# A fused encoder layer: moving waits, copies and one table load in the mix stage and first gate pair

## The chip, the cores and the metric

The kernel is one program on one core of a Trainium2 chip. The core has TensorE (PE: matmuls into PSUM, with the weight loads PEld beside them), VectorE (DVE), ScalarE (ACT), GpSimd (POOL) and SyncE (SP), whose queue issues nearly all DMA transfers here. The engines run their own instruction streams and meet at semaphores. The metric is the device time in microseconds, the median of several executions.

## The reference

One encoder layer in fp32 is computed for two sequences of 1024 and 512 tokens, width 1024:

```python
u = rms_norm(h, g_norm)
z = u @ w_in                      # q, k, v, attention gate, recurrent input, its gate
o_att = diff_attention(q, k, v, ...)      # 8 heads, softmax difference, rms_norm per head
o_lru = rg_lru_branch(xr, ...)            # conv, two gated scans
mix = concat([o_att * silu(g_att), o_lru * silu(g_lru)])
h = h + mix @ w_out
e = (p @ w_ple) * sigmoid(h @ w_pg)
h = h + rms_norm(e, g_ple)
```

## The kernel before

The 1536 tokens are 12 tiles of 128. Products are made from a high and a low fp32r part of each operand, three matmuls for one. The stages follow each other: projections, recurrent branch, attention (96 steps, the last near 745 us), then the mix stage and the gate stage, which the change touches.

In the mix stage, position n of twelve takes tile SEQ[n], SEQ = 0, 1, 2, 8, 9, 3, 10, 4, 11, 5, 6, 7. Its steps are these. SP's load_o(n) (L862) reads the tile's attention output from DRAM into one of two buffers o_in. square_o(n) on ScalarE (L1473) squares it, mean_square(n) on VectorE (L1982 to L1989) sums, scales and inverts, root_o and scale_o(n) on ScalarE (L1477, L1484) give O_n, with eight scalings. turn_o(n) on TensorE (L2474) transposes O_n. o_gate(n) on VectorE (L1996) multiplies with the gate Gt that load_mix(n) (L868) has fetched into its one buffer, mix_high(n) on ScalarE (L1468) and mix_low(n) on VectorE (L2003) split the result. mix_product(n) on TensorE (L2212 to L2214) is 24 matmuls with wa, and add_x(n) on VectorE (L2022) adds the residual row. For tiles 0 to 7 (HALF: eight positions, n = 0, 1, 2, 5, 7, 9, 10, 11) the recurrent half of the product was made in the attention stage and stored to hpart; SP loads it (load_hp) with x (load_x_again), and GpSimd adds them (add_half, L1119). For tiles 8 to 11 (WHOLE: n = 3, 4, 6, 8) TensorE makes that half here, from mf and wl (L2436 to L2438, half_tile, 12 matmuls each, two for a tile); the first of them, at n = 3, is made ahead. TensorE takes turn_o(n + 1) ahead of mix_product(n), and so ahead of the half tiles in it.

Beside this the gate's weights are prepared: load_wg (L814) fetches eight blocks of 512 KB of w_pg in two halves, gate_sum and gate_low on VectorE (L2026) and gate_high on ScalarE (L1488) form sums and high and low parts, one or two for a position, each of 128 x 2048 elements. The gate product is of Strassen's kind: for each of six pairs of tiles, seven products p1, p5, p6, p7, p3, p4, p2 (L2537 to L2540) in place of eight. TensorE keeps each sum in PSUM and ScalarE's copy_sum (L1596) saves p1, p5 and p6 before the next adds to the same bank. a11, a22, a12 and s1 to s4 are quarters of the transposed h and their sums; *_high on ScalarE (L1533, L1541, L1547, L1556) and *_low on VectorE and GpSimd (L1137) split them.

The order on each engine is written out by hand. A wait blocks all that stands behind it on its engine; the order of SP's queue (L918 to L964) is the order in which the transfers are requested. A pair's products wait as follows: p6 for the low part of s2, for the copy of p1 and for weights; p7 for the copy of p6. a22_high(0) waits for add_x(11), since a22 lies where hp_sb was. load_o(n) waits for scale_o(n - 2); load_o(3) also for the last store of attention output (store_o(1, 3), L779). In the lists for ScalarE (L1564) and VectorE (L2078) the loop over n goes through the positions.

Of the kernel before, what the change touches and what calls it, by code (L numbers as in the profile page):

```python
# [26 lines left out]
ACT = mybir.ActivationFunctionType  # L27
# [8 lines left out]
NT = T // P  # L36
NB = T // 512
HEADS, HV, HQ = 8, 64, 32
# [34 lines left out]
def encoder_layer(nc, x, x_t, p_in, g_norm, w_in, w_cols, norms, lams, rel_bias, onehot, chan, w_a, w_x,  # L73
# [20 lines left out]
    with ctx:  # L94
# [486 lines left out]
        def _(sp):  # L581
# [193 lines left out]
            def store_o(u, i):  # L775

                n_tok, first = UNITS[u]
                sp.wait_ge(o_done, 4 * i + 3 + u)
                sp.dma_start(o_tok[first:first + n_tok, ds(P * i, P)].rearrange("(t p) c -> p t c", p=P),  # L779
                             O_at[i % 2][:, first // P:(first + n_tok) // P, :]).then_inc(o_st[i % 2], 16)  # L780
# [24 lines left out]
            def store_hp(j):  # L805
                sp.wait_ge(hp_done, j + 1)
                sp.dma_start(hpart[j // 2 * P:(j // 2 + 1) * P, j % 2 * 512:(j % 2 + 1) * 512], hp[:, j % 2, :]
                             ).then_inc(hp_out[j % 2], 16)
                if j % 2 and j // 2 + 2 < NT:
                    load_mf(j // 2 + 2)  # L810

            def load_wg(half):
                for k in range(4 * half, 4 * half + 4):
                    sp.dma_start(wg_raw[:, k, :], w_pg[k * P:(k + 1) * P, :]).then_inc(wg_in[half], 16)  # L814
# [43 lines left out]
            def load_o(n):  # L858
                if n >= 2:
                    sp.wait_ge(fin["o_norm"], n - 1)  # L860
                t = SEQ[n]
                sp.dma_start(o_in[n % 2][:], o_tok[t * P:(t + 1) * P, :]).then_inc(fin[f"o_in{n % 2}"], 16)  # L862

            def load_mix(n):
                if n:
                    sp.wait_ge(fin["mixed"], n)
                t = SEQ[n]
                sp.dma_start(Gt[:], z_ch[P:, t * P:(t + 1) * P].rearrange("(c r p) t -> p c r t", r=3, p=P)[:, :, 2, :]  # L868
                             ).then_inc(fin["g_in"], 16)
# [57 lines left out]
            load_o(1)  # L927
            load_hp(0)
            load_hp(1)
            sp.wait_ge(s_mm, 2 * NSTEP)  # L930
            load_wg(1)
            store_hp(IN_STEPS - 2)
            load_mix(1)
            store_hp(IN_STEPS - 1)
            for b in range(2):
                sp.wait_ge(hp_out[b], 16 * IN_STEPS // 2)
            load_x_again(1)
            load_o(2)
            store_o(1, HEADS // 2 - 1)
            load_mf(10)  # L940
            for n in range(NT):
                if n == 0:
                    load_mix(n + 2)
                    sp.wait_ge(o_st[1], 16 * 4)
                if n + 3 < NT:
                    load_o(n + 3)
                if 1 <= n < NT - 2:
                    load_mix(n + 2)
                if 1 <= n < NT - 1:
                    load_x_again(n + 1)  # L950
                    if n + 1 in HALF and HALF.index(n + 1) >= 2:
                        load_hp(HALF.index(n + 1))
                if 1 <= n <= IN_DRAM:
                    store_h(n - 1)
                if n == 4:
                    load_mf(11)
                if n == 8:
                    sp.wait_ge(f_mm, 2 * NT)
                    for k in range(PC):
                        sp.dma_start(wp_raw[:, k, :], w_ple[k * P:(k + 1) * P, :]).then_inc(wp_in, 16)  # L960
                if n == 9:
                    load_p(0, 1)
                    load_p(0, 0)
# [222 lines left out]
        def _(act):  # L1186
# [327 lines left out]
            mix_high(0)  # L1514
            heads_out(2 * HEADS - 1)
            square_o(2)
            mix_high(1)

            def a21_copy(g):
# [42 lines left out]
                act.activation(p_hi[:, r, :, :], p_sb[:, r, :, :], ACT.Copy).then_inc(fin["p_hi"], 1)  # L1562

            for n in range(NT):  # L1564
                if n == 0:
                    root_o(2)
                    scale_o(2)
                if n + 3 < NT:
                    square_o(n + 3)
                if 1 <= n < NT - 1:  # L1570
                    mix_high(n + 1)
                if 1 <= n < NT - 2:
                    root_o(n + 2)
                    scale_o(n + 2)
                if n in (0, 1, 2, 3, 4, 6, 8):
                    gate_high({0: 0, 1: 1, 2: 2, 3: 3, 4: 4, 6: 5, 8: 6}[n])
                if n == NT - 3:
                    for k in range(PC):
                        act.wait_ge(wp_in, 32)
                        act.activation(wp_hi[:, k, :], wp_raw[:, k, :], ACT.Copy).then_inc(wp_hi_done, 1)  # L1580
# [4 lines left out]
            sum_high(0, 1, s3_raw, s3, "p7")  # L1585
            sum_high(0, 2, s1_raw, s1, "p5")
            sum_high(0, 3, s2_raw, s2, "p6")
            a22_high(0)
            a12_high(0)
            sum_high(0, 4, s4_raw, s4, "p3")  # L1590

            def copy_sum(g, name, ps, at, free):
                act.wait_ge(fin["g_mm"], START["g_mm"] + step_of(name, g))
# [23 lines left out]
            for g in range(PAIRS):  # L1617
                if g:
                    gate_sigmoid(g - 1, 3, sg[0][:, LEFT])
                copy_sum(g, "p1", left_ps[:], sg[0][:, LEFT], 0)  # L1620
                if g:
                    square_e(g - 1, 0)
                copy_sum(g, "p5", right_ps[:], sg[1][:, RIGHT], 1)
                copy_sum(g, "p6", left_ps[:], sg[0][:, RIGHT], 0)
                if g < LAST:
                    a21_copy(g + 1)
                gate_sigmoid(g, 1, sg[1][:, RIGHT])
                gate_sigmoid(g, 2, sg[0][:, RIGHT])
                if g == LAST:
                    break  # L1630
                a11_high(g + 1)
                sum_high(g + 1, 1, s3_raw, s3, "p7")
                left_sigmoid(g)
                a22_high(g + 1)
                sum_high(g + 1, 2, s1_raw, s1, "p5")
                sum_high(g + 1, 3, s2_raw, s2, "p6")
                square_e(g, 1)
                a12_high(g + 1)
                sum_high(g + 1, 4, s4_raw, s4, "p3")
                p_high(g + 1, 1)  # L1640
                p_high(g + 1, 0)
# [9 lines left out]
        def _(dve):  # L1651
# [397 lines left out]

            def gate_weights(n):  # L2050

                if n < 3:
                    gate_sum(n)
                if n == 3:
                    gate_low(wg_hi[:, TOP, LEFT], wg_lo[:, TOP, LEFT], wg_raw[:, TOP, LEFT], 1, 1)
                if n == 4:
                    gate_low(t1_hi[:], t1_lo[:], t1_raw[:], 2, 3)
                if n == 5:
                    gate_low(wg_hi[:, TOP, RIGHT], wg_lo[:, TOP, RIGHT], wg_raw[:, TOP, RIGHT], 4, 2)
                if n == 6:  # L2060
                    gate_low(wg_hi[:, BOTTOM, RIGHT], wg_lo[:, BOTTOM, RIGHT], wg_raw[:, BOTTOM, RIGHT], 3, 3)
                if n == 8:
                    gate_sum(3)
                    gate_low(t2_hi[:], t2_lo[:], t2_raw[:], 5, 4)
                if n == 9:
                    gate_low(wg_hi[:, BOTTOM, LEFT], wg_lo[:, BOTTOM, LEFT], wg_raw[:, BOTTOM, LEFT], 6, 4)
                if n == 10:
                    gate_low(t4_hi[:], t4_lo[:], t4_raw[:], 7, 4)
# [9 lines left out]
            for n in range(NT):  # L2078
                if 1 <= n < NT - 1:
                    o_gate(n + 1)  # L2080
                if n:
                    add_x(n - 1)
                if 1 <= n < NT - 1:
                    mix_low(n + 1)
                if n + 3 < NT:
                    mean_square(n + 3)
                gate_weights(n)

            def sum_three(g):
                dve.wait_ge(fin["t_act"], 4 * g + 1)  # L2090
# [112 lines left out]
        def _(pe):  # L2203
# [273 lines left out]
            def mix_product(n, between=None):  # L2477
                if n == 1:
                    pe.wait_ge(wt_done, NSTEP)
                    pe.wait_ge(o_done, 2 * HEADS)  # L2480
                if n == 2 or n >= 4:
                    pe.wait_ge(fin["h_done"], {2: 1, 4: 2, 5: 3}.get(n, n - 1))
                if n in WHOLE[1:]:
                    half_tile(2 * SEQ[n])
                    half_tile(2 * SEQ[n] + 1)
                pe.wait_ge(fin["m_lo"], n + 1)
                for b in range(2):
                    c = slice(b * 512, (b + 1) * 512)
                    mm = product(mix_bank(n)[:, b, :], [(m_hi[n % 2][:, k, :], m_lo[n % 2][:, k, :], wa_hi[:, k, c],
                                                         wa_lo[:, k, c]) for k in range(LC)], start=n in HALF)  # L2490
                    if between and b == 0:
                        between()
                mm.then_inc(fin["h_mm"], 1)
# [114 lines left out]
            pe.wait_ge(wa_lo_done, LC)  # L2608
            mix_product(0, second_tile)
            for n in range(1, NT - 1):  # L2610
                turn_o(n + 1)
                mix_product(n)
            turn_a21(0)
            turn_a11(0)
# [70 lines left out]
```

## Time and profile before

| | |
|---|---|
| median of 3 executions | 1032.72 us (1032.64 to 1032.97) |
| profiled execution | 1032.86 us, span 1031.1 us |
| TensorE busy | 991.2 us, 96% |
| VectorE, ScalarE, GpSimd busy | 671.5, 638.0, 483.5 us |
| chain that ended last | PE 70%, DVE 15%, issue 8%, ACT 3% |
| DMA | 154.55 MB, mean 150 GB/s |

Times in the rows are microseconds from the span's start. A row of the timeline has start, duration, engine, line, operation, what it writes and reads, and in brackets the idle time of the engine before it with what ended it. The last of the attention stage is near 745 us, the mix stage runs from there to 855 us, the gate stage to the end.

### The profile page before, as it was taken

How to read it: one execution, taken by the hardware profiler on the slowest of the kernel's cores; microseconds unless marked ns; L12 is line 12 of the kernel's file. 1: busy time of each engine (PE TensorE's matmuls, PEld its weight loads, DVE VectorE, ACT ScalarE, POOL GpSimd, SP SyncE). 2: the span in 40 equal slices, each digit the busy share in tenths (PEclk: the TensorE clock that was granted, in tenths of full speed). 3: DMA queues.
4: the chain of work that ended last, by engine and by line, in shares of the span. 5: the costliest groups of instructions: out<-in, count | busy, mean ns of one | idle time of the engine just before them, and what ended most of it. 6: DMA issues, size and time to landing. Idle time of an engine off the chain costs nothing.

```text
span 1031.1 us, 15665 instructions
## 1 busy us (share of the span) xinstructions
PE 991.2 (96%) x5720; PEld 786.0 (76%) x5720; DVE 671.5 (65%) x1118; ACT 638.0 (62%) x1050; POOL 483.5 (47%) x396
## 2 busy tenths in 40 slices
PE   8999999999999999989999999999988997999996
PEld 7867777777788888878777777777766886888875
DVE  4645857592583341579999999999857562444444
ACT  7748485846632232579999999999746442444442
POOL 1163343626666540155676677666610135554451
PEclk9999999999999999999999999999999998999998
DMA  9651543323256437669866657623557680122222
GB/s 346 260 151 36 174 148 103 118 82 133 75 178 185 134 102 207 199 167 241 210 174 172 176 160 180 155 64 139 176 175 235 206 274 10 41 92 81 84 72 82
DMA packets 106908, 154.55 MB, mean 150 GB/s; under 512 B 10312, under 2 KB 69192, under 8 KB 106824
## 3 DMA queue, kind: packets, MB, share of 16 engines
q1 hardware_dynamic: 106688, 153.55, 49.7%
q8 instruction: 46, 0.75, 0.3%
q14 instruction: 30, 0.25, 0.1%
q10 hardware_dynamic: 144, 0.00, 0.0%
HBM read 104.17 MB, written 46.20 MB: 146 GB/s over the span
## 4 chain that ended last, share of the span: by engine, by line
PE 70%; DVE 15%; issue 8%; ACT 3%; DMA 2%; POOL 2%; SPq 0%; DVEq 0%; ACTq 0%; POOLq 0%
DVE E_ L1905 10%; PE b_ps L2350 6%; PE b_ps L2352 6%; PE b_ps L2351 6%; PE b_ps L2212 6%; PE b_ps L2214 5%; PE b_ps L2213 5%; PE o_ps L2407 3%; PE s_ps L2363 3%; PE w_ps L2324 3%; PE uT_ps L2287 2%; PE left_ps L2537 2%; PE left_ps L2540 2%; PE left_ps L2539 2%; DVE ratio L1914 2%
## 5 line engine op out<-in xcount | busy, mean ns | idle before, releaser
L1387 ACT ACTIVATE E_<-E_,nmax 128x1024 f32<-128x1024 f32 (+1 forms) x184 | 186.5, 1018 | 13.2 <-DVE nmax L1905 13.2
L1905 DVE CUSTOM_DVE_ANT_0 E_<-s_ps,bias 128x1024 f32<-128x1024 f32 (+1 forms) x184 | 188.2, 1057 | 9.8 <-PE s_ps L2363 9.6
L1089 POOL TENSOR_TENSOR E_<-E_,ratio 128x576 f32<-128x576 f32 (+3 forms) x92 | 84.5, 919 | 92.8 <-DVE E_ L1921 92.8
L1092 POOL TENSOR_TENSOR E_<-E_ 128x576 f32<-128x576 f32 (+3 forms) x92 | 103.6, 1126 | 7.2
L2214 PE MATMUL b_ps<-u_hi,wA_lo 128*128 128x512 f32 x256 | 99.8, 390 | 0.0
L2363 PE MATMUL s_ps<-KL,QL 128*128 128x512 f32 x256 | 88.6, 430 | 8.1 <-DVE nmax L1905 8.0
L1402 ACT ACTIVATE WT<-w_ps 128x1024 f32<-128x1024 f32 (+1 forms) x96 | 83.5, 870 | 5.9 <-PE w_ps L2324 5.5
L2212 PE MATMUL b_ps<-u_hi,wA_hi 128*128 128x512 f32 x216 | 85.5, 396 | 0.0
L2324 PE MATMUL w_ps<-ident,E_ 128*128 128x128 f32 x624 | 83.5, 273 | 2.1 <-ACT WT L1402 2.0
L2324 PEld LDWEIGHTS w_ps<-ident,E_ 128*128 128x128 f32 x624 | 72.5, 140 | 15.2 <-issue 6.3
L2213 PE MATMUL b_ps<-u_lo,wA_hi 128*128 128x512 f32 x216 | 84.1, 389 | 0.0
L2407 PE MATMUL o_ps<-WT,V 128*64 128x128 f32 x1280 | 84.0, 278 | 0.0
L2407 PEld LDWEIGHTS o_ps<-WT,V 128*64 128x64 f32 x1280 | 68.5, 136 | 18.6 <-issue 18.6
L1000 POOL TENSOR_TENSOR rsq<-msq,neghalf 128x16 f32<-128x16 f32 x24 | 69.7, 2902 | 2.0
L1921 DVE SCALAR_TENSOR_TENSOR E_<-E_,ratio 128x448 f32<-128x448 f32 (+4 forms) x92 | 66.0, 718 | 3.2
L2350 PE MATMUL b_ps<-wB_hi,u_hi 128*128 128x512 f32 x168 | 66.8, 398 | 0.0
L2352 PE MATMUL b_ps<-wB_hi,u_lo 128*128 128x512 f32 x168 | 65.6, 390 | 0.0
L2351 PE MATMUL b_ps<-wB_lo,u_hi 128*128 128x512 f32 x168 | 65.4, 389 | 0.0
L1356 ACT ACTIVATE z_stage<-b_ps 128x512 f32<-128x512 f32 x24 | 14.3, 595 | 80.2 <-PE b_ps L2352 80.2
L1119 POOL TENSOR_TENSOR hp_sb<-hp_sb,x_rd 128x1024 f32<-128x1024 f32 x8 | 21.7, 2712 | 80.8 <-DMA hp_sb<-hpart 75.7
L1865 DVE TENSOR_REDUCE ssq<-z_stage 128x16 f32<-128x512 f32 x24 | 16.4, 683 | 66.0 <-ACT z_stage L1356 66.0
L2363 PEld LDWEIGHTS s_ps<-KL,QL 128*128 128x128 f32 x256 | 40.3, 189 | 20.7 <-DVE nmax L1905 17.2
(345 smaller groups left out, 2590.7 us busy)
## 6 DMA issues: line engine op xcount, KB each, us to landing
QL<-qk_t SPq DMA_DIRECT2D x32, 256.0 KB, 7.3
KL<-qk_t SPq DMA_DIRECT2D x32, 256.0 KB, 8.5
bias<-line_d SPq DMA_DIRECT2D x8, 960.0 KB, 11.8
x_sb<-in_x SPq DMA_DIRECT2D x12, 512.0 KB, 9.2
z_ch<-z_stage SPq DMA_DIRECT2D x24, 256.0 KB, 3.3
qk_t<-qh SPq DMA_DIRECT2D x24, 256.0 KB, 2.3
qk_t<-ql SPq DMA_DIRECT2D x24, 256.0 KB, 2.8
mf<-mix_t SPq DMA_DIRECT2D x24, 256.0 KB, 5.2
```

Of the source, the lines that this page charges most:

```text
L1092: gp.tensor_tensor(one, one, two, ALU.add).then_inc(w_gp, 1)
L1387: act.activation(e, e, ACT.Exp, bias=nmax[:, n % 5, c:c + 1], scale=-1.0, accum_out=sums[:, n % 5, c:c + 1]).then_inc(e_done, 1)
L1905: dve.tensor_tensor_reduce(weights_at(n)[:, c, 0:n_tok], s_ps[:, c, 0:n_tok], b[:, ::-1], -1.0, 3e38, ALU.add, ALU.min, nmax[:, n % 5, c:c ...
L2212: pe.matmul(dst, sh, mh, start=start and k == 0, stop=False)
L2213: pe.matmul(dst, sh, ml, start=False, stop=False)
L2214: mm = pe.matmul(dst, sl, mh, start=False, stop=k == n - 1)
L2324: mm = pe.transpose(w_ps[:, k, :], weights_at(n)[:, 0, k * P:(k + 1) * P], ident[:])
L2350: pe.matmul(dst, u_hi[:, b, k, c], wB_hi[g][:, k, :], start=k == 0, stop=False)
L2351: pe.matmul(dst, u_hi[:, b, k, c], wB_lo[g][:, k, :], start=False, stop=False)
L2352: mm = pe.matmul(dst, u_lo[:, b, k, c], wB_hi[g][:, k, :], start=False, stop=k == KC - 1)
L2363: mm = pe.matmul(s_ps[:, c, b * 512:(b + 1) * 512], q_tile(u, hh)[:, c, qt * P:(qt + 1) * P], k_tile(u, hh)[:, c, b * 512:(b + 1) * 512], ...
L2407: mm = pe.matmul(o_ps[HV * j:HV * j + HV, 0, pair * P:(pair + 1) * P], V_at[i % 2][:, first // P + k, HV * (head % 2):HV * (head % 2) + HV ...
```

## The change

- SP: load_o(2) goes from behind load_x_again(1) to right behind load_mix(1), ahead of two stores. store_o(1, 3) goes ahead of the waits on hp_out and load_x_again(1). load_wg(1), with its wait, goes from ahead of store_hp(14) into the loop at n = 0, behind load_o(3).
- ScalarE: one added activation, a Sqrt of one element for each partition, between square_o(2) and mix_high(1). In the loop mix_high(n + 1), root_o(n + 2) and scale_o(n + 2) stand ahead of square_o(n + 3), where the square stood first. In the first pair a22_high(0), a12_high(0) and sum_high(0, 4) go behind the copies of p1 and p5.
- VectorE: gate_sum(1) and gate_sum(2) go from n = 1 and 2 to n = 2 and 3, the first gate_low from 3 to 1; gate_weights(n) stands ahead of mean_square(n + 3).
- TensorE: at n = 4, 6 and 8 turn_o(n + 1) goes behind the half tiles, ahead of the rest of mix_product(n).

```diff
--- SP
             load_hp(1)
-            sp.wait_ge(s_mm, 2 * NSTEP)
-            load_wg(1)
             store_hp(IN_STEPS - 2)
             load_mix(1)
+            load_o(2)
             store_hp(IN_STEPS - 1)
+            store_o(1, HEADS // 2 - 1)
             for b in range(2):
                 sp.wait_ge(hp_out[b], 16 * IN_STEPS // 2)
             load_x_again(1)
-            load_o(2)
-            store_o(1, HEADS // 2 - 1)
             load_mf(10)
...
                     load_o(n + 3)
+                if n == 0:
+                    sp.wait_ge(s_mm, 2 * NSTEP)
+                    load_wg(1)
--- ScalarE
             square_o(2)
+            act.activation(mse[:, 0:1], neghalf[:, 0:1], ACT.Sqrt, scale=-2.0)
             mix_high(1)
...
             for n in range(NT):
-                if n == 0:
-                    root_o(2)
-                    scale_o(2)
+                if 1 <= n < NT - 1:
+                    mix_high(n + 1)
+                if n + 2 < NT:
+                    root_o(n + 2)
+                    scale_o(n + 2)
                 if n + 3 < NT:
                     square_o(n + 3)
-                if 1 <= n < NT - 1:
-                    mix_high(n + 1)
-                if 1 <= n < NT - 2:
-                    root_o(n + 2)
-                    scale_o(n + 2)
...
             sum_high(0, 3, s2_raw, s2, "p6")
-            a22_high(0)
-            a12_high(0)
-            sum_high(0, 4, s4_raw, s4, "p3")
...
                 copy_sum(g, "p5", right_ps[:], sg[1][:, RIGHT], 1)
+                if g == 0:
+                    a22_high(0)
+                    a12_high(0)
+                    sum_high(0, 4, s4_raw, s4, "p3")
                 copy_sum(g, "p6", left_ps[:], sg[0][:, RIGHT], 0)
--- VectorE
-                if n < 3:
-                    gate_sum(n)
-                if n == 3:
+                if n in (0, 2, 3):
+                    gate_sum((0, None, 1, 2)[n])
+                if n == 1:
                     gate_low(wg_hi[:, TOP, LEFT], wg_lo[:, TOP, LEFT], wg_raw[:, TOP, LEFT], 1, 1)
...
+                gate_weights(n)
                 if n + 3 < NT:
                     mean_square(n + 3)
-                gate_weights(n)
--- TensorE
                     half_tile(2 * SEQ[n] + 1)
+                    turn_o(n + 1)
...
             for n in range(1, NT - 1):
-                turn_o(n + 1)
+                if n not in WHOLE[1:]:
+                    turn_o(n + 1)
                 mix_product(n)
```

## Rows read from the trace of the kernel before

**Rows 1.** The page's first part: busy us, share of the span, instructions of each engine.

```profile
PE 991.2 (96%) x5720; PEld 786.0 (76%) x5720; DVE 671.5 (65%) x1118; ACT 638.0 (62%) x1050; POOL 483.5 (47%) x396
```

**Rows 2.** Timeline of TensorE: start, duration, line, operation, idle before and releaser.

```profile
765.06 0.65 PE L2474 MATMUL t_ps<-ident,O_n 128*128 128x128 f32 x4 [4.20 <-ACT O_n L1484]
...
782.25 0.66 PE L2474 MATMUL t_ps<-ident,O_n 128*128 128x128 f32 x4 [3.36 <-ACT O_n L1484]
...
836.49 0.60 PE L2474 MATMUL t_ps<-ident,O_n 128*128 128x128 f32 x4
...
842.52 0.60 PE L2474 MATMUL t_ps<-ident,O_n 128*128 128x128 f32 x4
...
867.58 0.77 PE L2537 MATMUL left_ps<-t_hi,s_hi 128*128 128x512 f32 x1 [5.53 <-issue]
```

**Rows 3.** Stretches: length, busy time (instructions) by engine, granted clock, DMA share, GB/s.

```profile
740.00:746.00 6.00, 6.00 (x54) 4.74 (x52) 3.59 (x3) 2.05 (x2) 5.24 (x5) 1.00 1.01 402
...
765.00:769.00 4.00, 3.94 (x13) 3.21 (x14) 3.37 (x5) 2.96 (x4) 0.00 (x0) 0.60 0.22 66
...
782.20:785.60 3.40, 3.35 (x11) 2.72 (x12) 3.40 (x3) 2.46 (x3) 0.00 (x0) 0.59 0.33 87
...
867.50:871.50 4.00, 3.92 (x9) 3.15 (x10) 0.00 (x0) 0.47 (x1) 0.84 (x1) 0.50 0.00 0
```

**Rows 4.** Timeline of ScalarE in the mix stage, same columns.

```profile
758.11 0.63 ACT L1473 ACTIVATE O_sq<-o_in 128x512 f32<-128x512 f32 x1 [8.76 <-DMA o_in<-o_tok]
760.81 0.63 ACT L1468 ACTIVATE m_hi<-mr 128x512 fp32r<-128x512 f32 x1 [2.06 <-DVE mr L1996]
761.46 1.28 ACT L1477 ACT_TABLE_LOAD   x1
...
778.90 0.63 ACT L1473 ACTIVATE O_sq<-o_in 128x512 f32<-128x512 f32 x1 [4.75 <-DMA o_in<-o_tok]
...
837.91 0.64 ACT L1468 ACTIVATE m_hi<-mr 128x512 fp32r<-128x512 f32 x1 [1.45 <-DVE mr L1996]
...
838.67 2.03 ACT L1484 ACTIVATE O_n<-o_in,rso 128x64 f32<-128x64 f32 x8
```

**Rows 5.** Timeline of SP's queue: start and duration of each issue of a transfer.

```profile
747.63 0.38 SPq L868 DMA_DIRECT2D Gt<-z_ch  x1
...
751.96 0.43 SPq L862 DMA_DIRECT2D o_in<-o_tok  x1
...
753.70 0.37 SPq L779 DMA_DIRECT2D o_tok<-O  x1
...
761.26 0.45 SPq L862 DMA_DIRECT2D o_in<-o_tok  x1
```

**Rows 6.** DMA issues of 736:739, 739.4:739.6, 753.6:754, 761.2:761.5: count, KB, us to landing.

```profile
wg_raw<-in_w_pg SPq DMA_DIRECT2D x4, 512.0 KB, 8.6
...
hpart<-hp SPq DMA_DIRECT2D x1, 256.0 KB, 9.0
...
o_tok<-O SPq DMA_DIRECT2D x1, 512.0 KB, 7.3
...
o_in<-o_tok SPq DMA_DIRECT2D x1, 256.0 KB, 3.1
```

**Rows 7.** VectorE's stretch (busy, clock, DMA, GB/s); timeline of GpSimd and VectorE at 743.

```profile
805.10:811.10 6.00, 5.62 (x7) 1.00 0.67 227
...
743.12 2.37 POOL L1119 TENSOR_TENSOR hp_sb<-hp_sb,x_rd 128x1024 f32<-128x1024 f32 x1
743.19 2.85 DVE L1974 TENSOR_TENSOR O_n<-o_in,rso 128x512 f32<-128x512 f32 x1 [2.37 <-POOL rso L1112]
```

**Rows 8.** Timeline of GpSimd and ScalarE in the first pair, same columns.

```profile
856.39 3.79 POOL L1137 TENSOR_TENSOR s_lo<-s_raw,s_hi 128x512 fp32r<-128x512 f32 x3 [1.59 <-ACT s_hi L1556]
...
860.13 2.39 POOL L1119 TENSOR_TENSOR hp_sb<-hp_sb,x_rd 128x1024 f32<-128x1024 f32 x1
...
866.89 0.59 ACT L1596 ACTIVATE sg<-left_ps 128x512 f32<-128x512 f32 x1
```

## The prediction

> **What bounds the kernel now.** Read the busy shares first: TensorE is busy 991.2 us of a span of 1031.1 [rows 1]. So only idle or slow stretches of TensorE can be won. Next read TensorE's timeline for rows with an idle time before them, from the last attention steps (735 us) to the end. Three are over 0.7 us. The turn of the third output tile waits 4.20 us for O_n, the turn of the fifth waits 3.36 us for O_n, and product p6 of the first pair starts after 5.53 us without a releaser that the profile names [rows 2]. Then read the stretches for the granted clock. Behind each of the three gaps the clock is at its lower level, 1.2 GHz, for part of the stretch: mean 0.60 over 4.0 us, 0.59 over 3.4 us, 0.50 over 4.0 us [rows 3]. TensorE stays busy there and does less, so a gap also costs 4.0 x 0.40 = 1.6, 3.4 x 0.41 = 1.4 and 4.0 x 0.50 = 2.0 us. The three together hold 13.1 us of idle time and 5.0 of slow clock, 18.1 us. All else in this part of TensorE's timeline is back to back.
>
> **The third tile (first gap).** ScalarE's rows show the order of the delay: square_o(2) waited 8.76 us for the transfer of o_in(2) and ran at 758.11, and behind it lie the VectorE chain, mix_high(1), a table load of 1.28 us, the root and eight scalings [rows 4]. The transfer was issued at 751.96, fifth after Gt(1) at 747.63 [rows 5]. The change issues it right behind Gt(1), at 748.05. A load of this size landed in 3.1 us [rows 6], so it lands at 751.2; even with the 9.0 us of a transfer behind 2 MB it would be there at 757.1. VectorE cannot take it before 753.7 (heads_scaled), and its three small steps end by 755. The extra Sqrt makes the table load run while ScalarE is idle until 758.1 [rows 4]. It fits in those 8.76 us, so I cost it at nothing; if a second load were to come behind it, that would be 1.28 us more.
> What is late next is the turn of tile 1 at 757.47, which is not moved. From a turn to m_hi is 1.42 us (836.49 to 837.91), and from m_hi's start to the end of O_n is 2.79 us (837.91 to 838.67 + 2.03) [rows 2, 4]. So m_hi(1) starts at 758.9 and O_n(2) ends at 761.7. TensorE runs out of work at 765.06 - 4.20 = 760.86. New gap: 0.85 us.
>
> **The fourth and fifth tiles.** A half-tile step of TensorE lasts 6.03 us (836.49 to 842.52) [rows 2], so the turn of tile 3 is due at 761.7 + 6.0 = 767.7. load_o(3) waits for the store of heads 6 and 7 (issued 753.70, landed 7.3 us later at 761.0, with three transfers beside it). One of these has now gone ahead and x_rd(1) comes behind, so the store no longer decides; mixed(2) at 758.9 does. The request leaves at 759.3 in place of 761.26 [rows 5]. In front of it are the two mf transfers of load_mf(10) and Gt(2), so I take 763.3 and not 759.3 + 3.1 = 762.4 [rows 6]. Where a square is what VectorE waits for, m_hi starts 2.7 us behind the square's start (758.11 to 760.81, with one turn between) [rows 4]; taking 2.6, m_hi(2) is at 765.9 and O_n(3) ends at 768.7: a gap of 0.95 us where there was none. Between 0.1 us (landing 762.4) and 2.4 us (landing 764.8).
> Behind load_o(3) now go the four loads of the gate weights, 2 MB, from 759.7. SP's queue stands 2.5 us longer, and load_o(4), load_mix(3), load_x_again(2), load_hp(2), store_h(0) and load_o(5) queue behind it. The rows price this: weights land 8.6 us after issue, and the 256 KB store behind them in the kernel before took 9.0, against 3.1 us for a free queue [rows 6]. The first weights were then behind 1.5 MB of other loads; now only Gt(2) and o_in(3) are ahead. 2.1 MB at the 402 GB/s of that time [rows 3] are 5.2 us. From 762.9, when o_in(3) is through, that puts the end of the weights at 768.1 and o_in(4) at 769.3, with its own 0.6 us and 0.6 to the semaphore (estimate; 771.4 with the full 9.0 from 762.4). square_o(4) starts with ScalarE free at 768.7, so 769.3; m_hi(3) is at 771.9 and O_n(4) ends at 774.7, both by the same two spans. Turn 4 is due at 768.7 + 6.0 = 774.7. Gap 0 to 0.1, up to 2.1 with the late landing. The 3.36 us gap there came from square_o(5) standing ahead of mix_high(3) and waiting 4.75 us for its transfer [rows 4]; with squares last, a late o_in(5) meets a step with 5.5 us more to give, because tile 9's half products now run ahead of the turn.
> Sum: 4.20 + 3.36 + 1.6 + 1.4 = 10.6 us go, 0.85 + 0.95 + 0.05 = 1.85 come, gain 8.7.
>
> **The later tiles.** At three whole tiles (positions 4, 6, 8) the turn moves behind 24 half products, 5.5 us nearer to its product. From turn to O_n of the next tile is 1.42 + 2.79 = 4.2 us against 6.03 us: 1.8 us of cover at positions 4 and 6. At position 8 VectorE has two gate steps of 2.25 us each between that turn and mean_square(11), which was ahead of them before: the chain is 12.4 us for two steps of 12.1. I take 0.2 us. SP's load_mix waits for that turn's o_gate, so loads of x, hp and w_ple leave up to 5.5 us later at positions 4, 6 and 8. The last additions of GpSimd (2.39 us each [rows 8]) may then hold add_x(10): 0 to 1.5 us, I take 0.3.
>
> **The first pair (third gap).** Follow the rows back. p6 starts at 867.58, right behind ScalarE's copy of p1 at 866.89. p1 had ended by 858.9; the copy stood behind a22_high, which waited for add_x(11), which waited for GpSimd's addition at 860.13 to 862.52, which stood behind three s_lo from 856.39 [rows 2, 8]. The change puts copies p1 and p5 ahead of a22_high. p6 then needs the third s_lo (856.39 + 3.79 = 860.2), copy p1 (859.6) and the end of p5 at 862.05: no gap. Next late are the embedding product at 864.9 (its p_lo ends by 864.0) and p7 at 868.1, which needs the copy of p6; ScalarE gets to that at 867.0, after the same high parts as before, and is done at 867.5. Cover 0.6 us. Gain 5.53 + 2.0 = 7.5 us; all of p6 to the end moves with it. If the cover fails, what a22_high lacks falls on p7.
>
> **Sum.** 8.7 - 0.2 - 0.3 + 7.5 = 15.7 us. The profiled execution took 1032.86 us (span 1031.1), 0.14 over the median of 1032.72. 1032.72 - 15.7 = 1017.0 us. Ends of the unknown costs: with no new gap at all 1014.6; with the late values at tiles 3 and 4 (1.5 + 2.0) and add_x(10) (1.2) 1021.7.
>
> **Rivals.**
> A. The 2 MB in the queue make a new gap. For it: 9.0 against 3.1 us [rows 6], and eight transfers behind. Against: a step to spare. o_in(4) 2.1 us later and o_in(5) or hp(2) late enough for one more 2 us, with one clock drop of 1.6 [rows 3]: 1017.0 + 5.5 = 1022.5. Chance 0.14.
> B. The reordered copies only shift the wait to p7, because GpSimd's last addition lands late (it follows all SP loads that now leave later). Then the 7.5 are not won: 1024.5. Chance 0.08.
> C. VectorE becomes the bound, and the kernel is slower. In a half-tile step with a gate step it is busy 5.62 of 6.00 us [rows 7], and mean_square now stands behind the gate step, so that nothing is left in between. The place is GpSimd's addition of hp and x: at 743.12 it ran 2.37 us, and VectorE's O_n begun at 743.19 took 2.85 us, until it was over [rows 7], where this size takes 0.69. If in each of the eight half-tile steps an addition met a VectorE subtraction first, a step would last 5.62 + 2.39 = 8.0 us: 8 x 2.0 = 15.8 us, and with three clock drops of 1.5 the time is 1017.0 + 20.3 = 1037.3. It makes the kernel slower from 2.0 us per step on. Against it: the additions now fall on PSUM reads and reductions in most steps. Chance 0.04. The Trainium skill, SBUF — State Buffer, section "Who interferes with whom", states this as a rule: a VectorE operation with two SBUF inputs and a GpSimd one that reads SBUF exclude each other, and the second waits for the whole first. By that rule the moved subtractions (two SBUF inputs) speak against this change, with the time of C at full overlap; the row at 743.19 agrees.
> The forecast itself: 0.72. Something else: 0.02.
>
> **How the numbers follow.** The forecast's own range is 1014 to 1020. With rival A and the late bounds it reaches to 1023; B and C, 0.12, are left out with what lies under 1013.8. A measurement of this kernel can tell about 0.2% (2 us) from no change. The forecast, A and B are all faster: 0.93. Within 0.2% needs B with A: 0.03. Slower: 0.04.
>
> **What would show it.** Right: m_hi(1) near 758.9 with no table load behind it; turn 2 at 761.7 with 0.9 us idle before it; turns 3 and 4 with idle times under 1 us each; full granted clock from 760 to the end of the pair stage; p6 directly behind p5; the turn at the first whole tile 5.5 us behind its half products' start. Wrong: an O_sq row that waits for o_in over 3 us at tile 4; an idle time before p7 or the embedding product; VectorE's m_lo or gate rows of over 2.5 us; an idle time before the turns of tiles 10 and 11.

## The result

| | us | ratio to the kernel before, 95% interval |
|---|---|---|
| kernel before | 1032.68 | |
| changed kernel | 1017.84 | 0.9853 (0.9834 to 0.9873) |
| the same once more, another chip run | 1017.93, beside 1031.86 | 0.9869 (0.9849 to 0.9888) |

The forecast was 1017.0 us, the range 1013.8 to 1023.0. The time fell by 14.8 us in the first set and by 13.9 in the second; 15.7 were forecast. The profile below is of one execution of the second set, 1020.3 us with a span of 1018.5. (The first set has four executions, and the one profiled took 1975.09 us, with TensorE busy for 99% of it at a recorded clock of 1.00, and cannot be compared: the median of 1017.84 counts it, the ratio is that of the other three, and their median is 1017.26, 15.4 us below the kernel before.)

The first part of the page after, beside [rows 1], has 2.8 us less of busy TensorE and a shorter span:

```profile
span 1018.5 us, 15666 instructions
PE 988.4 (97%) x5720; PEld 783.9 (77%) x5720; DVE 672.2 (66%) x1118; ACT 638.5 (63%) x1051; POOL 486.9 (48%) x396
```

The timeline of TensorE after, the rows that answer to [rows 2], in brackets the idle time before one: the turns of positions 2, 3 and 11, the turn of h for a12, p6, the turn behind it, and p7. The turn of position 3 is new among them; L2511 turns h for the first pairs.

```profile
761.32 0.66 PE L2474 MATMUL t_ps<-ident,O_n 128*128 128x128 f32 x4 [0.87 <-ACT O_n L1485]
...
770.19 1.12 PE L2474 MATMUL t_ps<-ident,O_n 128*128 128x128 f32 x4 [2.62 <-ACT O_n L1485]
...
836.69 0.66 PE L2474 MATMUL t_ps<-ident,O_n 128*128 128x128 f32 x4
...
850.28 0.66 PE L2511 MATMUL t_ps<-ident,h_sb 128*128 128x128 f32 x4 [0.45 <-DVE a_lo L2026]
...
856.36 0.39 PE L2538 MATMUL left_ps<-t_hi,s_hi 128*128 128x512 f32 x1
...
861.88 0.60 PE L2511 MATMUL t_ps<-ident,h_sb 128*128 128x128 f32 x4
862.23 0.48 PE L2538 MATMUL left_ps<-wg_hi,s_hi 128*128 128x512 f32 x1
```

p6 starts at 856.36, directly behind p5 (the row at 867.58 in [rows 2] had 5.53 us before it), and the turn behind p6 and its embedding product follows after 5.52 us. The timeline of ScalarE after, its table load and the two squares that waited, against [rows 4]:

```profile
751.00 0.63 ACT L1474 ACTIVATE O_sq<-o_in 128x512 f32<-128x512 f32 x1 [2.04 <-DMA o_in<-o_tok]
751.65 1.28 ACT L1518 ACT_TABLE_LOAD   x1
...
758.48 0.63 ACT L1469 ACTIVATE m_hi<-mr 128x512 fp32r<-128x512 f32 x1 [5.33 <-DVE mr L1996]
759.02 0.19 ACT L1478 ACTIVATE rso<-rso 128x8 f32<-128x8 f32 x1
759.25 2.02 ACT L1485 ACTIVATE O_n<-o_in,rso 128x64 f32<-128x64 f32 x8
764.87 0.63 ACT L1474 ACTIVATE O_sq<-o_in 128x512 f32<-128x512 f32 x1 [3.60 <-DMA o_in<-o_tok]
...
768.12 2.02 ACT L1485 ACTIVATE O_n<-o_in,rso 128x64 f32<-128x64 f32 x8
```

The square of tile 2 runs 7.1 us earlier than before, the table load lies in idle time, and O_n(2) ends at 761.27 with the turn at 761.32. But the square of tile 3 now waits 3.60 us for its transfer, and O_n(3) ends at 770.14. TensorE had been idle since 767.57: 2.62 us. Stretches of the kernel after, as in [rows 3], with us, the busy time of TensorE, its weight loads, VectorE, ScalarE and GpSimd, the granted clock, the DMA share and GB/s: this gap, what follows, and the rest up to the end of the mix stage.

```profile
767.50:770.10 2.60, 0.07 (x1) 0.00 (x0) 2.60 (x3) 2.57 (x10) 0.00 (x0) 0.99 0.83 290
770.10:773.50 3.40, 3.31 (x10) 2.83 (x11) 3.22 (x6) 2.78 (x4) 0.00 (x0) 0.50 0.95 286
773.50:855.00 81.50, 81.00 (x374) 65.50 (x374) 52.73 (x62) 41.87 (x103) 25.07 (x11) 1.00 0.66 222
```

So one slow stretch is left, 3.4 x 0.50 = 1.7 us, where there were three. The transfers behind the gap, against [rows 6], are o_in(3) issued at 758.94, Gt(2) at 758.48, o_in(4) at 761.56 and the last store of heads at 753.30, with KB and us to landing:

```profile
o_in<-o_tok SPq DMA_DIRECT2D x1, 256.0 KB, 5.9
...
Gt<-z_ch SPq DMA_DIRECT2D x1, 256.0 KB, 5.4
...
o_in<-o_tok SPq DMA_DIRECT2D x1, 256.0 KB, 9.1
...
o_tok<-O SPq DMA_DIRECT2D x1, 512.0 KB, 5.2
```

### The profile page after: what moved, and what is told of

Same layout as the page of the kernel before. It is cut to its first block, busy times and chain, and to the rows that moved or that the text cites. A ratio compares the mean times of both kernels' runs of the same rounds, so it can differ in the third digit from the quotient of the medians.

```text
span 1973.3 us, 15666 instructions
## 1 busy us (share of the span) xinstructions
PE 1963.0 (99%) x5720; PEld 1239.4 (63%) x5720; DVE 671.7 (34%) x1118; ACT 652.2 (33%) x1051; POOL 471.0 (24%) x396
## 4 chain that ended last, share of the span: by engine, by line
PE 99%; DVE 0%; ACT 0%; issue 0%; DVEq 0%; POOL 0%; POOLq 0%
PE s_ps L2363 8%; PE o_ps L2407 8%; PE w_ps L2324 8%; PE b_ps L2352 6%; PE b_ps L2351 6%; PE b_ps L2350 6%; PE b_ps L2212 6%; PE b_ps L2213 6%; PE b_ps L2214 6%; PE left_ps L2540 2%; PE uT_ps L2287 2%; PE left_ps L2538 2%; PE left_ps L2541 2%; PE right_ps L2541 2%; PE h_ps L2212 2%; PE h_ps L2214 2%
## 5 line engine op out<-in xcount | busy, mean ns | idle before, releaser
L2214 PE MATMUL b_ps<-u_hi,wA_lo 128*128 128x512 f32 x256 | 172.6, 674 | 0.0
L2324 PE MATMUL w_ps<-ident,E_ 128*128 128x128 f32 x624 | 169.0, 439 | 0.0
L2407 PE MATMUL o_ps<-WT,V 128*64 128x128 f32 x1280 | 157.8, 444 | 0.0
L2363 PE MATMUL s_ps<-KL,QL 128*128 128x512 f32 x256 | 153.6, 718 | 0.0
L2213 PE MATMUL b_ps<-u_lo,wA_hi 128*128 128x512 f32 x216 | 145.8, 675 | 0.0
L2212 PE MATMUL b_ps<-u_hi,wA_hi 128*128 128x512 f32 x216 | 145.3, 673 | 0.0
L2350 PE MATMUL b_ps<-wB_hi,u_hi 128*128 128x512 f32 x168 | 114.9, 684 | 0.0
L2214 PEld LDWEIGHTS b_ps<-u_hi,wA_lo 128*128 128x128 f32 x256 | 75.4, 294 | 41.7 <-issue 39.2
L2212 PEld LDWEIGHTS b_ps<-u_hi,wA_hi 128*128 128x128 f32 x216 | 65.0, 301 | 53.2 <-issue 50.4
L2213 PEld LDWEIGHTS b_ps<-u_lo,wA_hi 128*128 128x128 f32 x216 | 64.3, 298 | 33.4 <-issue 30.8
```

Source lines behind the costliest of these rows:

```text
L2212: pe.matmul(dst, sh, mh, start=start and k == 0, stop=False)
L2213: pe.matmul(dst, sh, ml, start=False, stop=False)
L2214: mm = pe.matmul(dst, sl, mh, start=False, stop=k == n - 1)
L2324: mm = pe.transpose(w_ps[:, k, :], weights_at(n)[:, 0, k * P:(k + 1) * P], ident[:])
L2350: pe.matmul(dst, u_hi[:, b, k, c], wB_hi[g][:, k, :], start=k == 0, stop=False)
L2363: mm = pe.matmul(s_ps[:, c, b * 512:(b + 1) * 512], q_tile(u, hh)[:, c, qt * P:(qt + 1) * P], k_tile(u, hh)[:, c, b * 512:(b + 1) * 512], ...
```

## Experiments

Each is compared with the kernel before, run beside it on the same chip. The theory is the prediction's: three gaps and the clock behind them are what is won. Rivals A (the 2 MB of gate weights in the queue), B (the copies only move the wait) and C (VectorE becomes the bound) stand against it. Where an edit is to the changed kernel, "the whole" is that kernel. The sets ran on different chips. The kernel before took 1031.86 us beside the first four of the kernels below, 1032.36 beside the next four, 1033.02 beside the three after them and 1032.33 beside the last, and within a set its executions lie up to 4.9 us apart. So across sets the gains over the kernel before are what is compared (the whole: 13.9 us), and differences of 1 to 2 us are not read as effects. Each kernel has one trace, and what a trace shows is that one execution.

**The whole change again.** (Run whole.)

> The whole change once more, for its profile. My theory: 1017.0 us; idle time of TensorE 0.85 us before the turn of tile position 2, 0.95 us (0.1 to 2.4) before position 3, under 0.1 (up to 2.1) before position 4, 0.2 before position 11, none before p6, and the granted clock at its upper level from 760 us to the end of the pair stage. The rival in which the 2 MB of gate weights hold the queue: a gap of over 2 us before position 4 with a stretch of lower clock behind it, 1022 us. The rival in which the copies shift the wait: idle time before p7.

Measured 1017.93 us. The gap before turn 2 was 0.87 us, before turn 3 2.62, before turn 4 none, before turn 11 about 0.2 (836.69 where 6.03 us behind 830.44 is 836.47), before p6 and p7 none. A wait that I had not seen stood before the turn of a12, 0.45 us. Rival B's mark is absent. The gap of over 2 us with a stretch of lower clock, which was to be rival A's mark at position 4, came at position 3.

**The first pair's copies alone.** The kernel before with this edit is pair_only:

```diff
             sum_high(0, 3, s2_raw, s2, "p6")
-            a22_high(0)
-            a12_high(0)
-            sum_high(0, 4, s4_raw, s4, "p3")
...
                 copy_sum(g, "p5", right_ps[:], sg[1][:, RIGHT], 1)
+                if g == 0:
+                    a22_high(0)
+                    a12_high(0)
+                    sum_high(0, 4, s4_raw, s4, "p3")
```

> The kernel before with only the three high parts of the first pair put behind the copies of p1 and p5. My theory: the gap of 5.53 us before p6 and the slow clock of 2.0 us behind it go, 7.5 us: 1025.2. The first two gaps stay at 4.20 and 3.36. If the wait only shifts to p7: 1032.7.

Measured 1024.82 against 1031.86: 7.0 us, ratio 0.9931 (0.9911 to 0.9952). The gap before p6 is gone from the timeline of TensorE and the first gap stands nearly as before, 3.93 us (the second 3.49):

```profile
764.38 0.66 PE L2475 MATMUL t_ps<-ident,O_n 128*128 128x128 f32 x4 [3.93 <-ACT O_n L1484]
```

**Everything else alone.** The whole with this edit taken back is mix_only.

> The change without the reordered copies of the first pair. My theory: 8.7 - 0.5 = 8.2 us are won, 1024.5, with the gap of 5.5 us before p6 still there. If the parts are worth less together than alone, the sum of the two single gains is over the gain of the whole.

Measured 1025.51: 6.4 us, ratio 0.9938 (0.9919 to 0.9957). In the timeline of TensorE the gap before p6 is back, 5.56 us:

```profile
861.17 0.77 PE L2537 MATMUL left_ps<-t_hi,s_hi 128*128 128x512 f32 x1 [5.56 <-issue]
```

7.0 + 6.4 = 13.4 us, and the whole gave 13.9. Within the intervals the parts add up. The pair's part is the larger one, and the mix stage fell short of the forecast's 8.2.

**Gate weights in their old place.** Run wg_early is the whole, with

```diff
             load_hp(1)
+            sp.wait_ge(s_mm, 2 * NSTEP)
+            load_wg(1)
             store_hp(IN_STEPS - 2)
...
-                if n == 0:
-                    sp.wait_ge(s_mm, 2 * NSTEP)
-                    load_wg(1)
```

> The whole change, but the second half of the gate weights requested in its old place, ahead of the hpart stores. It tells what the 2 MB cost where they stand now. My theory: with them gone from behind load_o(3), o_in(4) lands 5 us earlier, but turn 4 waits for the chain of squares that starts at turn 3 either way, so the time falls by 0 to 0.5 us against the whole change (1016.5 to 1017). If the 2 MB make a gap of their own, it falls by 2 us or more.

Measured 1017.64 us, ratio 0.9860 (0.9841 to 0.9880): no difference from the whole that the timing can tell. In its timeline the gap before turn 3 is 1.52 in place of 2.62, with no slow stretch behind it, and that before the turn of a12 is 1.34 in place of 0.45 (VectorE waited 2.35 us for gpB, see below); o_in(3) landed at 763.99 in place of 764.85. Of the 1.10 us saved in one place 0.89 were waited for in the other. The 1.10 us cannot be put down to the 2 MB: in gain_late (below), with the 2 MB where the whole has them, the gap is 1.72 us. The two rows, first of wg_early (this kernel), then of gain_late:

```profile
769.33 0.65 PE L2473 MATMUL t_ps<-ident,O_n 128*128 128x128 f32 x4 [1.52 <-ACT O_n L1484]
...
769.42 0.66 PE L2475 MATMUL t_ps<-ident,O_n 128*128 128x128 f32 x4 [1.72 <-ACT O_n L1485]
```

**load_o(3) first.** Run o3_first is the whole, with SP's order

```diff
             store_o(1, HEADS // 2 - 1)
+            sp.wait_ge(o_st[1], 16 * 4)
+            load_o(3)
+            load_mix(2)
             for b in range(2):
                 sp.wait_ge(hp_out[b], 16 * IN_STEPS // 2)
             load_x_again(1)
             load_mf(10)
             for n in range(NT):
-                if n == 0:
-                    load_mix(n + 2)
-                    sp.wait_ge(o_st[1], 16 * 4)
-                if n + 3 < NT:
+                if 1 <= n and n + 3 < NT:
                     load_o(n + 3)
```

> The whole change with load_o(3) and load_mix(2) ahead of load_x_again(1) and load_mf(10) in SP's queue. In the trace of the whole change o_in(3) took 5.91 us to land behind x_rd(1), two mf transfers and Gt(2), and turn 3 waited 2.62 us. If what stands ahead in the queue is the cause, it lands in 3 to 4 us, by 762, the gap before turn 3 falls under 0.3 us, no stretch of lower clock is left, and 1.5 to 3.5 us are won where a drop is avoided (1015 to 1016). If the 2 MB behind it are the cause, it stays over 1.5 us.

Measured 1021.29 us, ratio 0.9890 (0.9870 to 0.9909): 11.1 us are won, 2.9 less than by the whole. The two intervals overlap; on the same chip in the same set the whole with only the wait for the gains moved took 1017.45 us, 3.8 us less. Half of the expectation held. o_in(3) landed in 2.7 us and the gap before turn 3 is gone. But the next load, behind the 2 MB, took 9.7 us, the square of tile 4 waited 5.76 us for it, and the gap came back larger before turn 4. The DMA issues of o_in(3) and o_in(4) in o3_first, with KB and us to landing:

```profile
o_in<-o_tok SPq DMA_DIRECT2D x1, 256.0 KB, 2.7
...
o_in<-o_tok SPq DMA_DIRECT2D x1, 256.0 KB, 9.7
```

And in the timeline of the same kernel the square that waited and turn 4:

```profile
771.73 0.63 ACT L1474 ACTIVATE O_sq<-o_in 128x512 f32<-128x512 f32 x1 [5.76 <-DMA o_in<-o_tok]
...
777.04 1.11 PE L2474 MATMUL t_ps<-ident,O_n 128*128 128x128 f32 x4 [4.03 <-ACT O_n L1485]
```

This is rival A's mechanism, in full view once the gap ahead of it no longer covers it (the next but one experiment takes the 2 MB away, and the gap goes). In the whole change o_in(4) lands just as late (9.1 us), but turn 3 is then 2.6 us late itself, so turn 4 does not wait. The 2 MB cost so little there because something else was late first. One thing this edit does not separate: it moves o_in(3) away both from what stood ahead of it and from the 2 MB behind it.

**The wait for the gains later.** The row below is from the timeline of VectorE in the whole. It waited for gpB, the gain row of the last norm, which is not used before the first pair's end.

```profile
848.17 0.69 DVE L2026 TENSOR_TENSOR s_raw<-t_ps,a_raw 128x512 f32<-128x512 f32 x1 [1.32 <-DMA gpB<-in_g_ple]
```

The edit on VectorE (run gain_late):

```diff
-            dve.wait_ge(gain_in, 32)
             sum_three(0)
...
                     joined(g - 1, 3, "p2", right_ps[:], sg[0][:, LEFT])
+                    if g == 1:
+                        dve.wait_ge(gain_in, 32)
                     scaled_e(g - 1, 1)
```

> The whole change with VectorE's wait for the gains gpB moved from ahead of the first pair's sums to the first use. In the trace of the whole change VectorE waited 1.32 us for this transfer, and the turn of a12 waited 0.45 us for a_lo. If the transfer is the cause, both go and 0.3 to 0.5 us are won in TensorE's timeline (less than the timing can tell). If the chain through add_x(10) is as late, the 0.45 stay.

Measured 1017.45 us, ratio 0.9865 (0.9849 to 0.9881). The wait and the 0.45 us before the turn of a12 are gone; the gain, 14.9 us, differs from the whole's by less than the runs scatter.

**The three together.** load_o(3) first, weights in their old place, late wait for the gains (run best).

> Both of these, with the second half of the gate weights in its old place ahead of the hpart stores (as in the run before, where that left the time unchanged). If the three terms add up, no gap of TensorE over 0.9 us is left in the mix stage and at the first pair: 0.87 before turn 2 and nothing else. 1018 - 2.6 - 0.5 = 1015, and down to 1013.5 where the clock drop of 1.6 was in the median. If the loads crowd each other again it stays at 1017 to 1018.

Measured 1015.62 us (1015.33 to 1015.98), ratio 0.9840 (0.9826 to 0.9855). Only 0.87 us before turn 2 is left in the mix stage. o3_first and this kernel ran in one set and differ by 5.7 us, with intervals that do not touch. They differ in the place of the weights and the wait for the gains; the second removed 0.45 us where it stood alone, so the place of the weights is worth about 5 us here. Their traces agree: a gap of 4.03 us and a slow stretch of 1.7 are gone. In the whole change the same place was worth nothing that could be measured.

**Without the added Sqrt.** Run no_sqrt is the whole, with

```diff
-            act.activation(mse[:, 0:1], neghalf[:, 0:1], ACT.Sqrt, scale=-2.0)
```

> The whole change without the added Sqrt of one column. The table load of 1.28 us comes back between m_hi(1) and the root. My theory: turn 2 waits 2.15 us in place of 0.87, but turn 3 is bound by o_in(3) and not by this, so its gap shrinks by the same 1.28 us: the time stays within 0.5 us. If the table load had a longer cost (2.66 us by the page ScalarE: Activation LUTs of the Trainium skill, section What ACT_TABLE_LOAD costs, which counts a drain with it), turn 2 would wait 3.5 us.

Measured 1018.3 us, ratio 0.9865 (0.9850 to 0.9880), no difference from the whole. Rows of its timeline, ScalarE and turn 2 of TensorE:

```profile
758.93 0.63 ACT L1469 ACTIVATE m_hi<-mr 128x512 fp32r<-128x512 f32 x1 [6.71 <-DVE mr L1995]
759.58 1.28 ACT L1478 ACT_TABLE_LOAD   x1
760.88 0.21 ACT L1478 ACTIVATE rso<-rso 128x8 f32<-128x8 f32 x1
...
763.19 1.12 PE L2473 MATMUL t_ps<-ident,O_n 128*128 128x128 f32 x4 [2.29 <-ACT O_n L1485]
```

The load costs 1.28 us and the step behind it starts at once: the gap is 2.29 us, 1.4 more than with the Sqrt, and not 3.5. No gap is left before turn 3, which is due 3.1 us later: 1.4 for the longer gap and 1.7 for a slow stretch behind turn 2. So what came later in one place was paid out of the next gap, as expected, and by more than the 1.28 us expected.

**The square first on ScalarE.** Run square_first is the whole, with the old order in the loop:

```diff
+                if n == 0:
+                    root_o(2)
+                    scale_o(2)
+                if n + 3 < NT:
+                    square_o(n + 3)
                 if 1 <= n < NT - 1:
                     mix_high(n + 1)
-                if n + 2 < NT:
+                if 1 <= n < NT - 2:
                     root_o(n + 2)
                     scale_o(n + 2)
-                if n + 3 < NT:
-                    square_o(n + 3)
```

> The whole change, but in ScalarE's loop the square of position n + 3 again ahead of mix_high and the root and scalings. My theory: square_o(5) waits for o_in(5), which lands near 778, and holds m_hi(3) and O_n(4), so turn 4 waits about 5 us and a stretch of lower clock follows: 4 to 7 us over the whole change, 1022 to 1025. If the order on ScalarE did not matter once the requests are early, the time stays at 1018.

Measured 1023.6 us, ratio 0.9909 (0.9892 to 0.9925): 9.4 us are won, 4.5 less than by the whole, and 5.3 less than by the next kernel, which ran beside it. The size was right and the place wrong by one tile: it is square_o(4), not square_o(5), that holds m_hi(2) and O_n(3), and turn 3 waits, as its timeline shows.

```profile
768.95 0.63 ACT L1474 ACTIVATE O_sq<-o_in 128x512 f32<-128x512 f32 x1 [3.36 <-DMA o_in<-o_tok]
769.49 0.61 ACT L1469 ACTIVATE m_hi<-mr 128x512 fp32r<-128x512 f32 x1
...
772.30 1.12 PE L2477 MATMUL t_ps<-ident,O_n 128*128 128x128 f32 x4 [5.84 <-ACT O_n L1485]
```

**The turns at whole tiles early.** Run turn_early is the whole, with turn_o(n + 1) again ahead of the half tiles at positions 4, 6 and 8.

```diff
                     half_tile(2 * SEQ[n] + 1)
-                    turn_o(n + 1)
...
-                if n not in WHOLE[1:]:
-                    turn_o(n + 1)
+                turn_o(n + 1)
```

> The whole change, but at positions 4, 6 and 8 the turn of the next tile again ahead of the half products. In the trace of the whole change O_n(5) ended at 783.25 while product 3 ended near 782.1: turn 5 would wait 1 to 1.5 us, the other two nothing, and the last turns lose their 0.2. So 0.5 to 1.5 us slower, near what the timing can tell. If the cover of 5.5 us was needed at all three places, 3 us or more.

Measured 1018.28 us, ratio 0.9860 (0.9846 to 0.9875). There is one gap of 0.70 us more, before turn 5, and the gain of 14.7 us is not distinguishable from the whole's. So this part of the change is not shown to be worth anything here.

**mean_square ahead of the gate step.** Run gates_after is the whole, with VectorE's two steps in the old order.

```diff
-                gate_weights(n)
                 if n + 3 < NT:
                     mean_square(n + 3)
+                gate_weights(n)
```

> The whole change, but VectorE's mean_square(n + 3) again ahead of the gate step. VectorE then waits for the square with the gate step behind it: o_gate(3) starts 2.3 us later and turn 4 waits about 2.3 us, with a clock drop of 1.6 at most; at position 8 the 0.2 us before turn 11 change little. 1 to 4 us slower: 1019 to 1022. If VectorE has room either way, 1018.

Measured 1023.05 us, ratio 0.9906 (0.9883 to 0.9929): 10.0 us are won, 4.0 less than by the whole and 4.8 less than by the kernel with the early turns, which ran beside it. The interval just overlaps the whole's and does not touch that kernel's. The time is 1 us over the highest that I had written. gate_sum(0), 2.3 us, already stands behind the wait of mean_square(3), so turn 3 and not turn 4 waits, 4.02 us; turn 11 waits 1.77 us, since the two gate steps at position 8 now begin only when the square of tile 11 is there (at 831.29, against 827.44 in the whole). The two turns in its timeline:

```profile
771.29 1.12 PE L2474 MATMUL t_ps<-ident,O_n 128*128 128x128 f32 x4 [4.02 <-ACT O_n L1485]
...
839.47 0.66 PE L2474 MATMUL t_ps<-ident,O_n 128*128 128x128 f32 x4 [1.77 <-ACT O_n L1485]
```

Against the whole's trace these two gaps are 1.4 and 1.5 us longer, 3 us together; the rest of the difference in the medians no trace explains.

**Turn 1 ahead of the second half tile.** On top of the three together (run best_turn1):

```diff
             def second_tile():
-                half_tile(IN_STEPS + 1)
                 turn_o(1)
+                half_tile(IN_STEPS + 1)
```

> The version with load_o(3) first, the gate weights in their old place and the late wait for the gains, and on TensorE the turn of tile 1 ahead of the 12 half products of tile 8's second half instead of behind them. My theory: turn 1 comes 2.7 us earlier, so m_hi(1) and O_n(2) do, and the last gap in the mix stage, 0.87 us before turn 2, goes; what is late next is o_in(3), which lands at 759.7: 1015.6 - 0.9 = 1014.7. If O_n(2) is held by something else (the square or the mean of tile 2), the gap stays and the time is 1015.6.

Measured 1014.88 us (1013.68 to 1014.89), ratio 0.9826 (0.9799 to 0.9852). No gap of TensorE is left from the attention's end to the second pair but 0.2 us before p5. The gain over the kernel before is 17.5 us against 16.7 for the three together; a difference of 0.7 us, about what was expected, but within the scatter.

Not tried alone are load_o(2) ahead of the stores, the moved last store of attention output and the new places of gate_sum and gate_low. For the first, the rows of o_in(2) and O_n(2) in the result stand as evidence.

## Why the prediction was right, point by point

- **What bounds the kernel**: right. Add up TensorE's idle times of 0.15 us and more from 745 to 880 us and what the lower clock costs there: 18.7 us in the kernel before, 5.6 in the whole, 0.2 in best_turn1. Taken from the span, they leave 1011.4 to 1013.4 us in all thirteen traces, so the gains and losses are those of these stretches to within 2 us. The parts add up too (7.0 + 6.4 against 13.9).
- **The first gap**: right, 0.87 us left (forecast 0.85), m_hi(1) at 758.48 (758.9). That the Sqrt costs nothing is right. That it is worth something here is not shown: without it the time is the same, and the 1.4 us go into the gap before turn 3.
- **The fourth tile**: the term that was mis-sized. The forecast took 0.95 us, at most 2.4; measured were 2.62 and, in the other kernels in which nothing but this load held turn 3, 1.72 (gain_late), 2.19 (mix_only) and 2.69 (turn_early). The step that failed is the landing of o_in(3), put at 763.3, 4.0 us behind its request: it took 5.9 us and landed at 764.85. x_rd(1), two mf transfers and Gt(2) stand ahead of it. I had counted them at 0.9 us over the 3.1 of a free queue; with the weights early it took 4.6 us, 1.5 over, and 2.7 with these transfers put behind it. What stands behind I had counted at nothing, and that is neither confirmed nor refuted: with the 2 MB behind it the load took 4.5 to 6.0 us in seven traces, without them 4.6 in one.
- **The clock**: the forecast had no stretch of lower clock left. One of 1.7 us came in the profiled execution. It does not come in each: in the profiled executions of gain_late, wg_early and turn_early there is none, behind gaps of 1.72, 1.52 and 2.69 us. How many of the whole's other executions had one is not known. In the first set the mean granted clock of an execution goes with the time (0.999, 0.998 and 0.996 at 1016.71, 1017.26 and 1018.41 us), in the second it does not (0.997 at 1017.80, 0.998 at 1018.06).
- **The fifth tile**: no gap, as forecast, but for another reason than the one given. The landing of o_in(4) was 770.68, 1.4 us behind the forecast and near its late bound of 771.4; it did no harm because turn 3 was late too: O_n(4) ended at 775.97, where turn 4 would have been due at 774.7 with turn 3 on the forecast's time (an estimate: 1.3 us of gap). The 0.6 us to the semaphore in the forecast of this landing stand in no row.
- **The later tiles**: 0.2 us at position 11 as forecast. The 0.3 at add_x(10) were measured as 0.45 us before the turn of a12, but the cause was another one: not GpSimd's addition, but VectorE's wait for gpB. The forecast did not list this load among those that leave later.
- **The first pair**: right, 7.5 forecast, 7.0 measured alone. p6 has no gap and p7 none (862.23, behind the turn at 861.88).
- **Sum**: against the profiled execution, 0.87 + 2.62 + 1.7 + 0.2 + 0.45 = 5.8 us stand where the forecast had 2.35, 3.5 us more; 1032.86 - 15.7 + 3.5 = 1020.7, and it took 1020.3. The medians are 2.4 to 3.0 us below this execution, the slowest of its four. That they lie only 0.3 to 0.9 us over the forecast is in part luck: the term of tile 3 and the clock were 3.4 us too small in the one execution that can be read. That the faster ones had a smaller gap there and no slow stretch, as gain_late's trace has (2.8 us in all, 1017.3 us), is likely and not shown.
- **Rival A**: did not decide here, but is real: 4.03 us before turn 4 in o3_first. Its time is a sum of 2.1 + 2 + 1.6, which is 5.7 and not the 5.5 that stands there. **Rival B**: refuted by the whole's trace, with no idle time before p7, and by mix_only: 1025.51 us without the reordered copies, 1017.93 with them. (pair_only cannot refute it, since SP's loads are not later there.) **Rival C**: its lock is seen, once at a cost. GpSimd's addition from 833.53 to 835.94 held VectorE's m_lo, which ended 0.56 us behind it and takes 0.69 us elsewhere, as the timeline of the whole shows:

```profile
833.53 2.41 POOL L1120 TENSOR_TENSOR hp_sb<-hp_sb,x_rd 128x1024 f32<-128x1024 f32 x1 [15.13 <-DMA hp_sb<-hpart]
...
834.87 1.63 DVE L2003 TENSOR_TENSOR m_lo<-mr,m_hi 128x512 fp32r<-128x512 f32 x1
```

It costs 0.94 us of VectorE and none of TensorE. More often it is GpSimd that takes longer: four of its eight additions, which take 2.4 us elsewhere, last 3.18 to 4.55 us in the whole, two in the kernel before. Such an addition holds no turn in this trace. VectorE is far from being the bound in eight steps, but gates_after shows how little is needed: its gate steps behind the wait in place of ahead of it cost 4 to 5 us in all.

## What to carry to other kernels

Cost a moved transfer by all that stands ahead of it in the queue at its new place, and the loads that leave later because of it; a queue's delay that one gap hides comes back in the next when the first is closed. On an engine that works in order put a step that waits for a transfer last in its round, and a copy that TensorE needs first. When one part of a change shows no effect alone, try it again with its neighbours mended: the old place of the gate weights was worth nothing in the changed kernel and about 5 us with load_o(3) early.

## What the runs showed of the hardware

A load of 256 KB took 2.7 to 3.1 us from issue to landing in a free queue, and 4.6 us (o_in(3) in wg_early) behind x_rd(1), two mf transfers and Gt(2). The load that followed the 2 MB of weights took 7.3 to 9.7 us (o_in(4) in no_sqrt 7.3, in o3_first 9.7). Whether a load in flight is slowed by what is requested behind it these runs leave open: in the same queue, with the 2 MB requested 0.5 us behind it, o_in(3) took 5.9 us in the whole, 6.0 in turn_early, 5.0 in gain_late and 4.5 in no_sqrt.

The granted clock does not follow the length of a gap alone. In the stretches below the granted clock is the number before the last two. The first is of no_sqrt, from the turn behind a gap of 2.29 us: the lower level, 1.2 GHz.

```profile
763.10:766.30 3.20, 3.11 (x10) 2.64 (x11) 1.69 (x5) 2.46 (x3) 1.60 (x1) 0.50 1.04 412
```

The second is of turn_early, from the turn behind a gap of 2.69 us, a longer one: 2.4 GHz throughout.

```profile
770.70:776.00 5.30, 5.25 (x25) 4.35 (x26) 5.11 (x8) 4.65 (x11) 0.00 (x0) 1.00 0.98 316
```

It also stayed at 2.4 GHz after 1.72 us in gain_late, and went down after 2.62 us in the whole (0.50 from 770.10 to 773.50). What decides between them these runs do not show.
